# Five dense expert tiles instead of four and a half, four gathered ones, gather rings of five, and a second norm that starts from matmuls

## What is computed

```
h = layer_norm(ALPHA * x + mix, ln1_g, ln1_b)
f = peer_ffn(h, ...)                    # per token c:
    s1, s2 = q[:half] @ keys_1, q[half:] @ keys_2; top 16 of each; top 16 of their sums -> sc, eid
    g   = softmax(sc)                                     # 8 heads x 16
    act = gelu(h[c] . peer_u[eid])                        # one dot product of 1024 for each expert
    f   = sum over the 128 picks of (g * act) * peer_v[eid]
y = layer_norm(ALPHA * h + f, ln2_g, ln2_b)
```

## Time and profile before

| | us |
|---|---|
| runs | 4797.03, 4830.70, 4828.28; median 4828.28 |
| profiled execution: its own time | 4800.55 |
| its span, first to last instruction | 4799.0 |
| stages up to the end of retrieve | 0 to about 2412 |
| build_gates, with the store of its last block | about 2412 to 2641 |
| experts | about 2641 to 4704.6 |
| ln2_out | 4704.7 to 4799.0 |

### The profile page before, as it was taken

How to read it: one execution, slowest core, us unless ns; L and a number is a source line. 1 busy time by engine, 2 the same in 40 slices (tenths; PEclk the granted TensorE clock), 3 DMA queues, 4 the chain that set the end, 5 groups by cost and what they waited for, 6 DMA issues and landing times. The chain is left out here.

```text
span 4799.0 us, 64513 instructions
## 1 busy us (share of the span) xinstructions
PE 3962.5 (83%) x24889; PEld 3686.0 (77%) x24889; DVE 3043.2 (63%) x5862; ACT 1179.5 (25%) x2121; POOL 1759.1 (37%) x1228
## 2 busy tenths in 40 slices
PE   7897979798999897798066489888888888888882
PEld 7796969657999896687055488888888888888882
DVE  3332323212222234399888699989998999999984
ACT  1212121311111101143289122222222222222221
POOL 0000000000000002377500566666766666666644
PEclk8787879899999999888589699999999999999996
DMA  5433332252111244110024899999999999999973
GB/s 154 152 99 122 108 113 65 78 218 73 59 60 60 85 130 141 56 31 10 0 124 193 333 359 357 355 350 362 360 355 358 348 359 359 356 356 354 358 271 112
DMA packets 470701, 982.63 MB, mean 205 GB/s; under 512 B 49022, under 2 KB 267518, under 8 KB 467427
## 3 DMA queue, kind: packets, MB, share of 16 engines
q0 software_dynamic: 156704, 619.52, 34.6%
q1 hardware_dynamic: 312578, 355.11, 21.8%
q10 hardware_dynamic: 1152, 4.46, 0.2%
HBM read 901.43 MB, written 131.28 MB: 215 GB/s over the span
## 5 line engine op out<-in xcount | busy, mean ns | idle before, releaser
L1879 POOL DMA_INDIRECT u_row<-in_peer_u_dram,eid x512 | 785.1, 1533 | 703.1 <-DVE dots L1938 417.7
L59 PE MATMUL e_ps<-coef_h,v_h 128*128 128x288 f32 x2048 | 661.3, 323 | 243.6 <-DVE v_l L1907 199.4
L59 PE MATMUL e_ps<-hBh,u_h 128*128 128x288 f32 x2048 | 607.4, 297 | 62.8 <-DVE u_l L1900 62.8
L1954 DVE SCALAR_TENSOR_TENSOR f_row<-v_row,g_coef,f_row 128x1024 f32<-128x1024 f32 x508 | 650.9, 1281 | 6.1 <-DMA v_row<-in_peer_v_dram,eid 5.6
L1885 POOL DMA_INDIRECT v_row<-in_peer_v_dram,eid x512 | 573.1, 1119 | 197.4 <-issue 154.2
L59 PEld LDWEIGHTS e_ps<-coef_h,v_h 128*128 128x128 f32 x2048 | 414.8, 203 | 298.1 <-DVE v_l L1907 244.9
L60 PE MATMUL e_ps<-coef_l,v_h 128*128 128x288 f32 x2048 | 634.4, 310 | 0.0
L61 PE MATMUL e_ps<-coef_h,v_l 128*128 128x288 f32 x2048 | 632.1, 309 | 0.0
L1938 DVE CUSTOM_DVE_ANT_0 u_row<-u_row,h_row 128x1024 f32<-128x1024 f32 x512 | 620.9, 1214 | 10.1 <-DMA u_row<-in_peer_u_dram,eid 10.0
L61 PE MATMUL e_ps<-hBh,u_l 128*128 128x288 f32 x2048 | 607.0, 296 | 0.0
L60 PE MATMUL e_ps<-hBl,u_h 128*128 128x288 f32 x2048 | 606.9, 296 | 0.0
(11 more groups left out here) (282 smaller groups left out, 8469.9 us busy)
## 6 DMA issues: line engine op xcount, KB each, us to landing
u_raw<-in_peer_uT_dram SPq DMA_DIRECT2D x128, 512.0 KB, 9.0
v_raw<-in_peer_vQ_dram SPq DMA_DIRECT2D x256, 256.0 KB, 8.5
s_g<-gate_block SPq DMA_DIRECT2D x9, 4096.0 KB, 11.2
x_gate<-s_g SPq DMA_DIRECT2D x64, 576.0 KB
out_o_kv_sample_dram<-in_cache_kv_w_dram POOLq DMA_DIRECT2D x2, 16256.0 KB, 94.6
c_raw<-in_w_in_dram SPq DMA_DIRECT2D x40, 512.0 KB, 3.8
w_raw<-in_w_in_dram SPq DMA_DIRECT2D x96, 192.0 KB, 3.7
cache_v<-in_cache_vS_dram SPq DMA_DIRECT2D x8, 2304.0 KB
```

The source lines that it names most:

```text
L59: pe.matmul(out, lh, rh, start=first, stop=False)
L1879: pool.indirect_dma_start(urow[:, r % RING], None, io["peer_u"][0], bass.IndirectOffsetOnAxis(ap=eid[:, r:r + 1], axis=0)).then_inc(urow_i ...
L1954: dve.scalar_tensor_tensor(out=f, in0=vrow[:, r % RING], scalar=coef[:, s % 2, x:x + 1], in1=f, op0=ALU.mult, op1=ALU.add).then_inc(weighe ...
```

## The change

1. The gathered tiles are now the last four (t = 5 to 8: 448 tokens, the last tile with its 64 samples), the dense ones the first five (640 tokens). All widths made from TB grow from 576 to 640: matmuls of `activations` and `values` from 288 to 320 columns, gelu, `coefs`, `coef_rest`, `add` from 576 to 640 elements. build_gates makes 10 blocks. The gathered loop still has 512 `dot` and 512 `weigh`; in the last 128 of each, and in their gathers, 64 partitions are used.
2. The rings have 5 buffers instead of 6.
3. retrieve goes over the tokens in pieces of 320, 320 and 448 instead of 512, 288 and 288.
4. ln2_out is written anew: every h and f is loaded at once into buffers of its own; PE makes ALPHA*h + f in PSUM (h times a scaled identity, plus f times the identity or `acc` turned) up to four tiles ahead; DVE takes the statistics from PSUM one tile ahead, and makes the result in two instructions; ACT takes the root and issues the stores, which nothing waits for but the end. POOL does nothing.

```
-TA = GTILES * P
-TB = T - TA
-HCHUNKS = ((0, TA), (TA, TB // 2), (TA + TB // 2, TB // 2))
+DTILES = NT - GTILES
+TB = DTILES * P
+TA = T - TB
+HCHUNKS = ((0, TB // 2), (TB // 2, TB // 2), (TB, TA))
...
-    TILES = range(GTILES, NT)
+    TILES = range(DTILES)
...
-    RING = 6
+    RING = 5
...
             def fetch_u(r):
                 if r >= RING:
                     pool.wait_ge(dotted, r - RING + 1)
-                pool.indirect_dma_start(urow[:, r % RING], None, io["peer_u"][0],
-                                        bass.IndirectOffsetOnAxis(ap=eid[:, r:r + 1], axis=0)).then_inc(urow_in[r % RING], 16)
+                n = rows_of(DTILES + r // P)
+                pool.indirect_dma_start(urow[:n, r % RING], None, io["peer_u"][0],
+                                        bass.IndirectOffsetOnAxis(ap=eid[:n, r:r + 1], axis=0)).then_inc(urow_in[r % RING], 16)
...
+                n = rows_of(DTILES + t)
+                dve.tensor_tensor_reduce(urow[:n, r % RING], urow[:n, r % RING], hrow[:n, t % 2], 1.0, 0.0, ALU.mult, ALU.add,
+                                         dots[:n, s % 2, x:x + 1]).then_inc(dotted, 1)
...
+        @block.sync
+        def _(sp):
+            for i, t in enumerate(ORDER):
+                n = rows_of(t)
+                sp.dma_start(H[:n, t], io["s_h"][t * P:t * P + n]).then_inc(h_in[t], 16)
+                if t >= DTILES:
+                    sp.dma_start(F[:n, t - DTILES], io["s_f"][t * P - TB:t * P - TB + n]).then_inc(h_in[t], 16)
+                if i == 0:
+                    sp.dma_start(gain[:], io["ln2_g"].to_broadcast([P, D])).then_inc(consts, 16)
+                    sp.dma_start(bias[:], io["ln2_b"].to_broadcast([P, D])).then_inc(consts, 16)
+        @block.tensor
+        def _(pe):
+            pe.wait_ge(alpha_ready, 1)
+            for i, t in enumerate(ORDER):
+                n = rows_of(t)
+                if i >= NY:
+                    pe.wait_ge(centred, i - NY + 1)
+                pe.wait_ge(h_in[t], 32 if t >= DTILES else 16)
+                for a in range(2):
+                    cols = slice(a * 512, (a + 1) * 512)
+                    pe.matmul(ps[:n, i % NY, cols], scaled_id[:n, :n], H[:n, t, cols], start=True, stop=False)
+                    if t >= DTILES:
+                        m = pe.matmul(ps[:n, i % NY, cols], k["ident"][:n, :n], F[:n, t - DTILES, cols], start=False, stop=True)
+                    else:
+                        for j in range(4 * a, 4 * a + 4):
+                            m = pe.matmul(ps[:n, i % NY, j * P:(j + 1) * P], k["acc"][:, j, t * P:t * P + n],
+                                          k["ident"][:], start=False, stop=(j % 4 == 3))
+                m.then_inc(y_ready, 1)
+        @block.vector
...
+            def stats(i):
+                n, x = rows_of(ORDER[i]), i % 2
+                dve.wait_ge(y_ready, i + 1)
+                for a in range(2):
+                    dve.bn_stats(st[:n, x, 6 * a:6 * a + 6], ps[:n, i % NY, 512 * a:512 * (a + 1)])
+                dve.drain()
+                dve.bn_aggr(mv[:n, x], st[:n, x]).then_inc(var_ready, 1)
+            def finish(i):
+                t, x = ORDER[i], i % 2
+                n = rows_of(t)
+                dve.wait_ge(std_ready, i + 1)
+                dve.reciprocal(rstd[:n, x:x + 1], std[:n, x:x + 1])
+                dve.scalar_tensor_tensor(out=H[:n, t], in0=ps[:n, i % NY], scalar=mv[:n, x, 0:1], in1=gain[:n],
+                                         op0=ALU.subtract, op1=ALU.mult).then_inc(centred, 1)
+                dve.drain()
+                dve.scalar_tensor_tensor(out=H[:n, t], in0=H[:n, t], scalar=rstd[:n, x:x + 1], in1=bias[:n],
+                                         op0=ALU.mult, op1=ALU.add).then_inc(done, 1)
+            stats(0)
+            dve.wait_ge(consts, 32)
+            for i in range(NT):
+                if i + 1 < NT:
+                    stats(i + 1)
+                finish(i)
```

121 lines of the change are left out of this document (48 added, 73 removed).

## The result

The changed kernel takes 4870.3 us (median of six runs, 4865.2 to 4921.3). The kernel before, run six times beside it, takes 4811.4 us (4788.3 to 4830.7). The ratio is 1.016, with a 95% interval of 1.012 to 1.020: slower by 1.6%. (The two medians alone would give 1.012; the median of before falls into a gap of 29 us between its low and its high runs.) The forecast was 4893 us, the range 4842 to 4933.

The account below looks back on a forecast made before the run. The prediction took a loop of DVE and PE in the experts to bound the kernel. Build_gates +23.0, experts +79 and ln2_out -37 made +65 on a median of 4828.3: 4893 us, range 4842 to 4933.

Parts of the forecast that it names:

- What bounds the kernel: Experts stage: a loop of DVE and PE sets the pace, 62.03 us a turn; DVE never waits for a gathered row.
- The turn: Experts, one turn: +0.68 activations, +0.86 DVE work, +0.34 last values, +0.56 new waits; sum +2.44 us.
- waits at the adds: Values part of a turn: every second add waits 0.28 us for PE, two on the path, +0.56; bounds 0 and 1.1.
- The experts: Experts stage: 29 turns +70.8, PE's end +6.5, first turn +2; +79 us, bounds 63 and 97.
- The ring of five: Gathered rows in experts: five buffers cost 0, since some 16 us are left for landings of 13.5 us at most.
- ln2_out: Last stage: 94.3 us falls to 57, saved 37, DVE the bound at 4.4 us a tile; bounds saved 15 and 41.
- Rival 1: Experts: PE's growth and the new wait find slack, only DVE's 0.86 a turn stays; sum +15, 4843 us; chance 0.15.
- Rival 2: Experts: DMA is the limit, so fetching less gives 176 us less if nothing else bound, 4638 us; chance 0.04.
- Rival 3: Experts: five buffers are too few, DVE waits about 3 us a turn, +93 more, 4986 us; chance 0.05.
- rival 5: Experts: gathered rows of 64 partitions cost half, 150 us less; excluded by 1.221 and 1.211, no chance of its own.
- Rival 4: ln2_out: PE stays at half clock, saving only 15 us; 4915 us; chance 0.10.
- The median: Starting point: 4828.3 us, the median of the runs shown, 28 above the profiled execution's 4800.6; plus 65 gives 4893.

Follow-up runs that it names:

- e5: The changed kernel with TensorE's activations from e = 2 on covering 288 columns of each half instead of 320; 4886.5 us.
- e6: The changed kernel with TensorE's values covering 288 columns of each half instead of 320; 4868.3 us.
- e7: The changed kernel with VectorE's adds, coefs and coef_rest covering 576 tokens instead of 640; 4875.7 us.
- e8: The kernel before with the new ln2_out, plus a gathered row done in VectorE's wait for gelu; 4714.5 us, ratio to before 0.980.
- e12: The kernel before, its last quarter's gathers bringing 64 partitions instead of 128, laid in partitions 32 to 95; experts stage 2063.6 us.
- e10: The kernel of e8 with the dot product of one more row moved ahead of coef_rest and coefs; ratio to before 0.980.
- e2: The changed kernel with the old ln2_out, its tiles indexed for the new split; 4941.1 us, ratio to before 1.031.
- e9: The changed kernel with the same edit of the row order as e8; 4837.8 us, ratio to before 1.006.
- e3: The kernel before with rings of five gathered rows instead of six, nothing else; 4820.0 us.

## Why the prediction was right, and where its sizes were off

**What bounds the kernel.** Right. The loop of DVE and PE sets the pace: taking work from PE (e5, e6), from VectorE (e7) or filling VectorE's idle time (e8) moves the turn. Taking nearly two fifths of the DMA traffic away (e12) moves it by 0.1 us at most, 61.9 us against 62.03. e8 shows that the engines could give 374 GB/s where 357 were asked for, and e10 that the bound may not be far above.

**The turn, +2.44 forecast.** Measured +2.82 in most turns (64.85 against 62.03) and +2.35 in the few at the clock of 0.97. DVE's busy time in a turn grew from 58.1 to 59.4 us, where 16 instructions by 0.066 make 1.06; each grew by 0.066 to 0.068, and some 0.2 us of that growth stays without a name. The wait for gelu grew by 3.95 - 3.35 = 0.60, where the forecast had about 0.6. The waits at the adds grew by 1.41 - 0.44 = 0.97.

The forecast put 0.28 on every second add, twice. The pattern came as it said, but three times ahead of the last add and not twice, with 0.28, 0.21 and 0.20; the last add waits 0.28 more than before. In a turn at 0.97 (the first of the two shown of the last quarter) the adds wait 0.20, 0.20, 0.20 and 0.45, so they grew by 0.61 there, against 0.56 forecast. So the sum was right at 0.97 (2.35 to 2.41, forecast 2.44) and lacked a term at 0.95. That is the step that was mis-sized: the waits at the adds came to 0.97 instead of 0.56, because the prediction took PE's matmuls in the turn at full clock. Here are the three stretches after `values(1)` starts in the turn shown above (columns as before):

```profile
3400.90:3404.30 3.40, 3.27 (x12) 3.28 (x13) 3.40 (x6) 0.00 (x0) 2.65 (x3) 0.50 0.87 292
3404.30:3407.70 3.40, 3.40 (x18) 3.33 (x17) 3.12 (x5) 0.33 (x1) 2.62 (x3) 0.68 0.98 357
3407.70:3411.10 3.40, 3.17 (x22) 2.90 (x20) 3.40 (x6) 0.45 (x2) 2.35 (x2) 1.00 0.94 337
```

TensorE had stood idle for 3.96 us, its clock was then 0.50, 0.68 and 1.00, and the wait of 0.28 at 3407.31 lies right behind, one add earlier than the first wait in the turn at 0.97. With the order of waits shifted by one add, the last one gets 0.72 instead of 0.45, and that is most of the difference of the two turns. Turns of 64.41 us at 0.97 come in the second quarter of e2 as well, at 344 GB/s, so the shorter turns of the last quarter don't come from less DMA traffic. Before, turns at 0.94 and at 0.97 both took 62.03 us; those at 0.95 took 62.2 to 62.3. TensorE worked 5.9 us at half clock in one of these, and 4.4 us in one of 62.03 at 0.94. So a turn of before paid this cost only in the worst case, where the changed kernel pays it in most. That the clock is the cause is read from where the waits stand; no run holds the clock fixed. It is worth 0.47 us a turn here. In e9 a stretch of half clock costs 1.5 us, but there it lies 32 to 33 us after the first coefs and not 26 to 27, near the place that costs 1.5 us in e8 too.

**The experts, +79 forecast, +88.6 measured.** By the prediction's own parts: the 29 turns +80.7 (forecast 70.8), of which the three with a store +10.3 instead of 7.3; the last turn and the end +8.3 (forecast 6.5); the start and the first turn -0.4 (forecast +2). Of the 9.6 us too few, 9.9 are the turns' (3.0 of them in the three with a store, which differ by some us between kernels with the same code), 1.8 the end's and -2.4 the start's, up to rounding.

**The ring of five.** Right, 0: shown by e3, and in the changed kernel itself no wait of DVE between 2850 and 4700 us names a gathered row.

**build_gates.** Right: +23.7, and 23.0 for the block. retrieve: right, 0.

**ln2_out, -37 forecast, -41.7 measured.** Within the bounds (15 to 41) but for 0.7 us. The first load landed after 3.7 us (forecast 4.3), the first tile was ready 5.4 us after PE started (forecast 6), DVE took 4.1 us a tile and not 4.4: nine tiles by 0.3 is 2.9 of the 4.7 us. The 0.4 us put down for reciprocal and drains were too many.

**Rival 1** (growth absorbed, a turn under 63.5) did not come. **Rival 2** fell: with 0.70 of the engines' time instead of 0.97 (e12) the turn stays at 61.9 us, and with more to fetch (e8) it gets shorter. The forecast itself held that the last quarter's share would go down; in the changed kernel it stayed at 0.98 and 1.01, since its 64 rows lie in partitions 0 to 63. In the profiled execution that cost nothing; in e2 and e9, with the same gathers, one and two turns of 72.8 to 73.9 us. Of what it rested on, the Trainium skill's about 358 GB/s for a core (DMA: Bandwidth & Descriptors, Specifications), this case shows more: 374 GB/s over a turn of e8. The same page of the Trainium skill (Bandwidth, Measured) has 425 GB/s for one core that streams alone, and the trace goes with that side. Where the bound for this mix lies above 374, e10 leaves open. **Rival 3** and **rival 5** did not come. **Rival 4** did not come: TensorE's clock was 0.50 for 3.4 us and then 1.00 for 30.4 us.

**The median.** The prediction started from 4828.3 us, the higher of two clusters, though the profiled execution lay near the lower one. With six runs the median of before is 4811.4. The terms of the forecast, +65, from there make 4876; the measured median is 4870.3. That closeness is partly luck: two terms were off by 9.6 and 4.7 us and partly cancel, and the two medians fall differently between the clusters. The traces give +70.6, and the low runs of both kernels, compared alone, 4867.3 - 4792.7 = +74.6. So the change costs some 70 to 75 us, and the forecast of +65 was 5 to 10 us short.

## What to carry to other kernels

Give the price of an added column in a loop of two engines as its terms along the loop, at both clocks: what was hidden while one engine had slack stops being hidden when the other grows. To compare turns, hold the clock equal, and look where in the turn the low clock falls; the mean over the turn is not enough. Before moving work between engines, look at what waits in that loop already. Here one gathered row moved into a wait of 3.35 us took 56 us off the experts (about 1%, and 2% together with the new norm), where this split alone cost 2 to 3%. And test a suspected limit from both sides, by asking less of it and by asking more. In this kernel half a tile of gathered rows did better in partitions 32 to 95 than in 0 to 63, by one execution of each.

## What the runs showed of the hardware

- Gathers into partitions 0 to 63 took 63.9% of the DMA engines for 16.48 MB, into 32 to 95 45.0% for 16.81 MB, into all 128 71.8% for 33.44 MB, each in some 124 us. With the first, single turns took 66 to 77 us. A DMA share near 1 at 214 GB/s does not mean that so little is all the engines can move.
- TensorE's granted clock fell to 0.50 for some 84 us of prompt_attn in ten of fourteen profiled executions (0.50 to 0.54), and was 0.82 to 0.87 in the other four, with the same code. In the ten the stage ended at 971.0 to 984.6 us, in the four at 934.6 to 948.7, on average 35 us apart: half of what the change does.
- After an idle time of 3.96 us TensorE's clock was 0.50 in the first 3.4 us of the `values` that followed.
- 3.4 us at half clock cost a turn of e8 nothing when they lay 25 us after the first coefs (59.69 us), and 1.5 us when they lay 31 us after it (61.18 us), at the same mean clock of 0.97 and the same work. Why the stretch lay in different places in turns of one execution was not settled.
